# Routing a mixture-of-experts layer from un-normalised activations, with a rewritten slot search, first gather and w_out order

## What is computed

```
h = layer_norm(ALPHA * x + m @ wo, g1, b1)                      # 1024 wide
g_prob = softmax(h @ w_group + b_group)                         # 4 groups, top 1
e_logits = (h @ w_router + b_router)[chosen group]              # 4 experts, top 2
wts = softmax(top 2 logits) * g_prob[chosen group]
y = sum over 16 experts of combine[:, e] * (silu(h @ w_gate[e]) * (h @ w_up[e])) @ w_down[e]
out = layer_norm(ALPHA * h + y, g2, b2)
```

## Time and profile before

| | us |
|---|---|
| median of 3 timed runs | 973.34 |
| timed runs | 973.19, 973.34, 979.06 |
| profiled execution, its own time | 978.55 |
| its span | 976.7 |
| TensorE busy | 857.7 (88%) |
| VectorE busy | 544.1 (56%) |
| ScalarE busy | 438.2 (45%) |
| GpSimd busy | 163.3 (17%) |
| mean granted TensorE clock | 0.935 of full |

### The profile page before, as it was taken

How to read it: one execution, slowest core, us unless ns; L and a number is a source line. 1 busy time by engine, 2 the same in 40 slices (tenths; PEclk the granted TensorE clock), 3 DMA queues, 4 the chain that set the end, 5 groups by cost and what they waited for, 6 DMA issues and landing times.

```text
span 976.7 us, 13661 instructions
## 1 busy us (share of the span) xinstructions
PE 857.7 (88%) x5313; PEld 758.9 (78%) x5313; DVE 544.1 (56%) x622; ACT 438.2 (45%) x551; POOL 163.3 (17%) x137
## 2 busy tenths in 40 slices
PE   4999897889798999999998998368999999999930
PEld 4999896667588999999996676357888888888820
DVE  4121347656652332333334332828999999999927
ACT  3222322654643332233314112136878778788722
POOL 0094024312210000000000332100211112111012
PEclk9999999999978999999999997569999999999975
DMA  7323114700101312221224235778999999999744
GB/s 293 118 87 102 69 53 143 253 0 1 44 8 52 139 60 102 102 94 62 99 86 138 80 139 209 296 284 314 384 379 403 393 388 404 384 398 404 218 83 136
DMA packets 35530, 180.76 MB, mean 185 GB/s; under 512 B 3575, under 2 KB 11399, under 8 KB 19134
## 3 DMA queue, kind: packets, MB, share of 16 engines
q1 hardware_dynamic: 30246, 161.38, 43.4%
q0 software_dynamic: 5248, 18.91, 7.5%
HBM read 166.77 MB, written 17.94 MB: 189 GB/s over the span
## 4 chain that ended last, share of the span: by engine, by line
PE 79%; DVE 8%; DMA 4%; ACT 4%; issue 3%; POOL 0%; SPq 0%; POOLq 0%; ACTq 0%; DVEq 0%
PE ps L1024 8%; PE ps L1025 8%; PE ps L1026 8%; PE ps L1287 6%; PE ps L1289 6%; PE ps L1288 6%; PE ps L863 4%; PE ps L864 4%; PE ps L865 4%; PE ps L1314 3%; PE ps L1316 3%; PE ps L1315 3%; PE ps L1190 3%; PE ps L1217 2%; PE ps L1216 2%
## 5 line engine op out<-in xcount | busy, mean ns | idle before, releaser
L1681 DVE TENSOR_TENSOR elo<-eraw,ehi 128x2048 fp32r<-128x2048 f32 x96 | 218.2, 2291 | 29.9 <-ACT ehi L742 28.1
L742 ACT ACTIVATE ehi<-eraw 128x2048 fp32r<-128x2048 f32 x96 | 183.0, 1916 | 28.3 <-PE ps L1289 16.1
L1372 DVE TENSOR_TENSOR wlo<-raw,whi 128x2432 fp32r<-128x2432 f32 (+1 forms) x25 | 63.4, 2535 | 154.8 <-ACT whi L504 154.8
L1024 PE MATMUL ps<-xhi,whi 128*128 128x260 f32 x384 | 110.5, 288 | 3.5 <-DVE wlo L1546 3.5
L1025 PE MATMUL ps<-xhi,wlo 128*128 128x260 f32 x384 | 110.2, 287 | 0.0
L1026 PE MATMUL ps<-xlo,whi 128*128 128x260 f32 x384 | 110.1, 287 | 0.0
L1287 PE MATMUL ps<-ehi,xethi 128*128 128x512 f32 x256 | 103.1, 403 | 5.0 <-issue 5.0
L1289 PE MATMUL ps<-elo,xethi 128*128 128x512 f32 x256 | 101.3, 396 | 0.0
L1288 PE MATMUL ps<-ehi,xetlo 128*128 128x512 f32 x256 | 101.2, 395 | 0.0
L504 ACT ACTIVATE whi<-raw 128x2432 fp32r<-128x2432 f32 (+1 forms) x25 | 52.4, 2094 | 91.0 <-PE ps L1026 91.0
L1024 PEld LDWEIGHTS ps<-xhi,whi 128*128 128x128 f32 x384 | 74.3, 194 | 3.7 <-DVE wlo L1546 3.7
(11 more groups left out here) (324 smaller groups left out, 1874.9 us busy)
## 6 DMA issues: line engine op xcount, KB each, us to landing
eraw<-w_gate_in SPq DMA_DIRECT2D x32, 1024.0 KB, 13.2
eraw<-w_up_in SPq DMA_DIRECT2D x32, 1024.0 KB, 14.8
eraw<-w_down_in SPq DMA_DIRECT2D x32, 1024.0 KB, 14.3
raw<-wm_in SPq DMA_DIRECT2D x16, 1216.0 KB, 5.2
raw<-wz_in SPq DMA_DIRECT2D x8, 1024.0 KB, 5.9
raw<-wo_in SPq DMA_DIRECT2D x4, 1024.0 KB, 4.9
h_dram<-hall POOLq DMA_DIRECT2D x5, 416.0 KB, 3.4
f_dram<-h_dram SPq DMA_DIRECT2D x1, 2080.0 KB, 9.7
```

The costliest lines, as they stand in the source:

```text
L742: ac.activation(ehi[s % 3][:, :], eraw[s][:, :], ACT.Copy).then_inc(ehi_ok, 1)
L1024: pe.matmul(out, cols(whi[s], q), mh, start=k == 0, stop=False)
L1681: ve.tensor_tensor(elo[s % 3][:, :], eraw[s][:, :], ehi[s % 3][:, :].bitcast(F32), ALU.subtract)\
```

## The change

- **Router.** `ln1_g` and `ln1_b` are loaded as 16 rows of 128, transposed once, and multiplied into the router weights: `wgb[:, 0] = g * w`, `wgb[:, 1] = b * w`. Their sums over the 1024 channels come from 8 products; `wrt` becomes `g*w - mean`, `brow` the bias row. Since the mean is taken out of the weights, the logits of the un-normalised `hall` need only a factor 1/sigma per token, which `logit(t)` applies. TensorE transposes tile t as soon as it is summed (`h_sum`) in place of finished.
- **Order on TensorE.** Tiles 0 and 1 go through w_out together, k-block by k-block (`first_two`); the last tile is made in two column halves, with logits and transposes of tiles 2 to 4 in between (`halves_of_last`).
- **w_out.** VectorE's split of its second piece stands one step after the first, ahead of the rest of the last merge step.
- **Slot lists.** A slot is the rank itself, in 16 lists; `rowhot` is made in two halves; everything on overflow is taken out: the count (`overflow_count`) stands behind expert 1 on VectorE, the lists (`overflow_lists`) behind the branch.
- **Gain and bias of tile 4**, the two VectorE steps `lng`, `lnb`, stand behind the choice of the experts; the splits of expert 0's first weights stand behind the slot search. A Sigmoid of one column on ScalarE makes the table load earlier.
- **Loads.** One down piece comes early; of the rest of the pieces and the copy to `f_dram`, none is issued before the first gather has landed. The second gather waits for the first.

```diff
-            sp.wait_ge(h_sum, TT)
+            sp.wait_ge(h_sum, TT + 1)
+            sp.dma_start(rcon[:, :], a["route_consts"]).then_inc(rc_in, 16)
             expert_piece(2, 2, wu[0, 0], True)
-            sp.dma_start(rcon[:, :], a["route_consts"]).then_inc(rc_in, 16)
             for n in range(2):
                 expert_piece(6 + n, 6 + n, wu[1, n], True)
+            expert_piece(8, 8, wd[0, 0], True)
             sp.wait_ge(h_done, TT - 1)
             sp.wait_ge(h_last, 2)
+            sp.wait_ge(h_sent, 16 * TT)
             expert_piece(3, 3, wu[0, 1], True)
-            sp.wait_ge(lg_ps, TT)
-            sp.wait_ge(h_sent, 16 * TT)
+            sp.wait_ge(xe_in[0], 16)
             for n in range(2):
                 expert_piece(4 + n, 4 + n, wg[1, n], True)
-            for n in range(2):
-                expert_piece(8 + n, 8 + n, wd[0, n], True)
+            expert_piece(9, 9, wd[0, 1], True)
             expert_piece(10, 10, wg[2, 0], True)
-            sp.wait_ge(slc_seen, 2)
+            expert_piece(11, 11, wg[2, 1], True)
             sp.dma_start(f_dram[0:T, :], h_dram).then_inc(f_init, 16)
...
+            ac.wait_ge(h_ps, TT + 1)
+            esplit(0, 0, 16, True)
+            esplit(1, 1, 16, True)
...
             ac.activation(m2[:, :], m2[:, :], ACT.Exp).then_inc(r_exp, 1)
+            ac.activation(eone[:, :], con[:, C_ONE:C_ONE + 1], ACT.Sigmoid)
+            esplit(2, 2, 16, True)
...
+            pe.transpose(ps[:, 7, 0:2 * KD], gb16[:, :], ident[0:2 * KD, 0:2 * KD]).then_inc(fold_ps, 1)
             with pe.Fori(1, KD) as i:
                 merge(i)
 
+            pe.wait_ge(fold_ok, 2)
+            for k in range(KD):
+                last = pe.matmul(ps[:, 7, 64:104].rearrange("p (u n) -> p u n", u=2), con[:, C_ONE:C_ONE + P],
+                                 wgb[:, :, k, :], start=k == 0, stop=k == KD - 1)
+            last.then_inc(fold_ps, 1)
...
+            def first_two():
+                pe.wait_ge(m_hi, KD - 1)
+                pe.wait_ge(m_lo, KD - 1)
+                for k in range(KD):
+                    if k % 2 == 0:
                         pe.wait_ge(lo_split, N_O + k // 2 + 1)
...
+                    if k == KD - 1:
+                        pe.wait_ge(m_hi, KD)
+                        pe.wait_ge(m_lo, KD)
+                    for t in range(2):
+                        if k == 0:
+                            pe.wait_ge(m_step, 4 * (KD - 1) + 1 + t)
+                        block(t, k)
...
+            def halves_of_last():
+                t = TT - 1
+                mt = slice(t * TR, t * TR + TR)
+                pe.wait_ge(h_sum, t - 1)
+                for h in range(2):
+                    out = ps[0:TR, 2 * (t % 2) + h, :]
+                    for k in range(KD):
+                        if h == 1 and k == KD - 3:
+                            logits(t - 1)
+                            turn(t, 0)
                         pe.matmul(out, mhi[:, k, mt], wohi[:, k, h * 512:h * 512 + 512], start=k == 0, stop=False)
...
+                    last.then_inc(h_ps, 1)
+                    if h == 0:
+                        logits(t - 2)
+                        turn(t - 1)
...
+            def turn(t, half=None):
+                if half is None:
+                    pe.wait_ge(h_sum, t + 1)
                 else:
-                    pe.wait_ge(h_last, 2)
+                    pe.wait_ge(h_sum, t + half + 1)
                 if t:
                     pe.wait_ge(ht_out, t)
-                for k in range(KD):
+                for k in range(KD) if half is None else range(4 * half, 4 * half + 4):
                     last = pe.transpose(ps[:, 4 + k // 4, (k % 4) * TR:(k % 4) * TR + TR],
                                         hall[:, t, k * P:k * P + P], ident[0:TR, 0:TR])
...
+            first_two()
+            turn(0)
+            project(2)
+            logits(0)
+            turn(1)
+            project(3)
+            logits(1)
+            turn(2)
+            halves_of_last()
+            turn(TT - 1, 1)
...
+                    wo_split(1)
                 ve.wait_ge(m_step, 4 * i + 2)
...
+            ve.wait_ge(fold_ps, 1)
+            for n in range(2):
+                ve.tensor_tensor(wgb[:, n, :, :], wrt[:, :, :],
+                                 ps[:, 7, KD * n:KD * n + KD].rearrange("p (k a) -> p k a", a=1).broadcast_to([P, KD, 20]),
+                                 ALU.mult).then_inc(fold_ok, 1)
             with ve.Fori(1, KD - 1) as i:
                 merge(i, True)
             merge(KD - 1, False)
-            for j in range(1, 4):
+            for j in range(2, 4):
                 wo_split(j)
+            ve.wait_ge(fold_ps, 2)
+            ve.scalar_tensor_tensor(wrt[:, :, :], ps[:, 7, 64:84].rearrange("p (a n) -> p a n", a=1).broadcast_to([P, KD, 20]),
...
+            t = TT - 1
+            x, ls = hall[:, t, :], l1stat[t][0:TR]
+            ve.wait_ge(xrow_in[t % 2], 16 * (t // 2 + 1) + 16)
+            for h in range(2):
+                ve.wait_ge(h_ps, t + h + 1)
+                summed(t, slice(512 * h, 512 * h + 512))
+                ve.wait_ge(h_sum, t + h + 1)
+                stats(x, ls, h)
+                if h == 0:
+                    for n in range(TT - 2):
+                        logit(n)
+            ve.wait_ge(h_stat, 4 * t + 2)
+            ve.bn_aggr(ls[:, 12:14], ls[:, 0:12]).then_inc(h_stat, 1)
+            ve.wait_ge(h_stat, 4 * t + 3)
+            ve.tensor_scalar(ls[:, 14:15], ls[:, 13:14], EPS, None, ALU.add).then_inc(h_stat, 1)
+            logit(TT - 2)
+            ve.wait_ge(h_root, t + 1)
+            for n in range(4):
+                factor(n, ls, h_fac, 5 * t)
+            factor(4, ls, h_fac, 5 * t)
+            logit(TT - 1)
+            ve.wait_ge(rd, count[0])
...
+            ve.wait_ge(ln_in, 32)
+            ve.wait_ge(h_nrm, TT)
+            ve.tensor_tensor(x, x, lng[0:TR, :], ALU.mult).then_inc(h_last, 1)
+            ve.wait_ge(h_last, 1)
+            ve.tensor_tensor(x, x, lnb[0:TR, :], ALU.add).then_inc(h_last, 1)
...
+                                  rank.rearrange("p (a t) n -> p a t n", a=1).broadcast_to([TR, 2, TT, NE]), ALU.mult))
+            link(ve.tensor_reduce(slotf[:, :, :], picked[:, :, :, :], AX.X, ALU.add))
+            ve.tensor_tensor(chunkr[:, :, :, :], picks[:, :, :, :], wider(tokm[:, :, :], NE), ALU.mult)
+            ve.wait_ge(rc_in, 16)
+            row = rcon[0:TR, G_ROW:G_ROW + CAP]
+            for c in range(2):
+                ve.tensor_tensor(rowhot[:, c:c + 1, :, :], along(row, CAP, 1), wider(slotf[:, c:c + 1, :], CAP),
+                                 ALU.is_equal).then_inc(list_ok, 1)
...
+            link(ve.tensor_copy(rankc[:, :, :], rank))
+            link(ve.tensor_copy(tots[:, :], total))
+            ve.tensor_tensor(chunkw[:, :, :, :], picks[:, :, :, :], wider(w12[:, :, :], NE), ALU.mult).then_inc(list_ok, 1)
+            esplit(0, 0, True)
+            ve.wait_ge(slot_ps, 2)
+            ve.tensor_copy(wslot[:, 0:NE], ps[:, 7, P:P + NE]).then_inc(wslot_ok, 1)
+            link(ve.tensor_copy(ltri[:, :, :], rcon[0:TR, G_LT:G_LT + NE * NE].rearrange("p (a e) -> p a e", a=NE)))
             esplit(1, 1, True)
...
+            def overflow_count():
+                link(ve.tensor_scalar(oc[:, :], tots[:, :], float(CAP), None, ALU.is_gt))
+                for m in range(2, TT):
+                    link(ve.scalar_tensor_tensor(oc[:, :], tots[:, :], float(CAP * m), oc[:, :], ALU.is_gt, ALU.add))
+                link(ve.tensor_tensor(ocl[:, :, :], oc[:, :].rearrange("p (a e) -> p a e", a=1).broadcast_to([TR, NE, NE]),
...
             expert(0, 1)
+            overflow_count()
             with ve.Fori(1, NE // 2 - 1) as i:
...
+                if c == 1:
+                    gp.wait_ge(xe_in[0], 16)
                 gp.indirect_dma_start(out=xe[q][:, :], out_offset=None, in_=h_dram,
```

300 lines of the change are left out of this document (172 added, 128 removed).

## The result

The changed kernel takes **950.46 us** (median of four runs, 947.77 to 953.48) beside 973.27 for the kernel before (973.02 to 979.06): a ratio of 0.9746 over the runs, 95% interval 0.9712 to 0.978 (the two medians alone give 0.9766). The forecast was 952.5, with 944 to 961. The profiled executions took 978.55 and 953.48 us, 25.1 apart (spans 976.7 and 951.6, mean granted clock 0.935 and 0.950).

What follows compares the result with a forecast made beforehand. TensorE is the chain for 79% of the span, so edits pay only where it waits or runs at 1.2 GHz. Gains of 24.3 less 1.5 and 2 make 20.8 us, from 973.34 to 952.5, range 944 to 961.

Steps and rivals of the forecast that it cites:

- the second term: Last tile's sum to logits: 15.1 us before, 3.8 after, 11.3 us gained; the choice of experts keeps its 4.7 us.
- 1. w_out: Start and end of w_out: last tile's sum at 592.8 against 595.59, 3 us earlier (0 to 4.5).
- one spell at 1.2 GHz, as there is one before: In w_out, small products thin out the array's work; the low clock costs eight matmuls by 0.2, 1.6 us.
- no gap: Tiles 0 and 1 in w_out: pieces are split by the time their k-blocks are wanted; end at 547.7.
- 3. Choice to first expert: End of `both` to first expert matmul: 30.3 us before, 20.3 after, gather landing in 6; 10.0 us gained.
- rival (c): The first gather is not faster: 12.9 us stays, 4.1 less gained, time 956.6 us; chance 0.08.
- 4. The loop: Expert loop: the overflow count loses 1.5 us (0 to 2.8), supply of weight pieces 2 us (0 to 10).
- (a): Tighter fit: no 1.2 GHz spell in w_out, weight products at full clock, count and supply hidden; 945 us; chance 0.18.
- (b): Supply becomes the bound of the late experts: 8 to 10 us come back, time 959.5 us; chance 0.17.
- (d): Slower: all 26 us of transfer come back in the loop and the count costs 2.8; 978 us; chance 0.03.
- landmark signs: Among them: last sum near 593, logits 3.8 later, gather landing in 6, TensorE gap of 1 to 3 in expert 2.
- the signs that it would be wrong: TensorE waiting for `elo` over many experts, `h_dram` store or gather above 10 us, long 1.2 GHz in w_out.

Runs made afterwards that it cites:

- the control: The changed kernel run once more, unaltered: 950.31 us, ratio 0.9766 to the kernel before.

## Why the prediction was right, and where it was not

**It was right in total** (952.5 forecast, 950.46 measured): 20.8 us were forecast, the medians are 22.8 apart, and the changed part of the two profiles gained some 22.5. Part of the agreement is luck. w_out gave 2.15 us more than forecast and the search 1.65 less, and in the loop two misses of about the same size cancel. Only the second term held both in size and in mechanism.

**1. w_out: 3 us forecast, 5.15 measured; a size.** Counted from the merge step, the first matmul starts 5.76 us behind it; the forecast had 525.6 - 519.69 = 5.9. Tiles 0 and 1 then take 22.45 us (522.84 to 545.29, where the first transposes start) for 22.1. The difference is in the last part. The forecast put one spell at 1.2 GHz there, 1.6 us, and four tiles' logits at 1.64; the clock stayed at 1.00, and the logits took 1.40, 4 x 0.24 = 1.0 less. Together 2.6, of which some lost tenths take 0.4 back. The step that failed is "one spell at 1.2 GHz, as there is one before". The trace of before has in fact two spells of about eight matmuls in w_out: one from 539.2 to 542.6, behind the waits of 2.97 us and, for the last piece, 2.77; and one from 583.6 to 587, behind a tile's transposes, a wait for their copy and its logits (TensorE's timeline of before; the matmuls of the second row and its neighbours are 0.43 us apart):

```profile
581.10 1.64 PE L1234 MATMUL ps<-wrt,ht 128*104 128x20 f32 x16 [0.95 <-ACT ht L721]
...
584.40 0.63 PE L1215 MATMUL ps<-wohi,mhi 128*104 128x512 f32 x1
```

The changed kernel, with twice as many tiles' small products in w_out, has neither spell. It makes a tile's logits after the next tile's products, so that TensorE has no wait between transposes and logits; its start has no wait either, and the experiment that only starts late has a spell of thirteen matmuls. So the waits are what it lacks, and the small products it has. That a wait of 0.95 us was the cause of the second spell was not tried, and the same wait at 566.6 had no spell behind it. The step "no gap" held, but its reason was only half of it: the early landing of the last piece, on which the forecast rested it, costs nothing when undone alone, since the pairing of the tiles covers the same wait. Only with both undone do 6.0 us come back.

**2. Sum to logits: 11.3 forecast, 11.7 measured.** The logits are there 3.4 us behind the sum (forecast 3.8), and the choice takes the same 4.7. The experiments split the 11.7, if their parts can be added: 5.1 come from transposing what is not yet normalised; gain and bias, no longer ahead of the logits, are 2.5 (two steps of 1.23); 0.9 comes from putting tile 3's logits and half of tile 4's transposes among w_out's last products, which costs w_out 1.8; and what is left, 11.7 - 5.1 - 2.5 - 0.9 = 3.2, goes to the order in which tiles 2 to 4 are transposed and to the last sum by halves. That last part was not tried by itself.

**3. Choice to first expert: 10.0 forecast, 8.35 measured.** This is the step that failed in kind. "With the queue nearly empty ... landing 3.4 to 4 later ... It just misses being the limit": it took 8.24, and was the limit. SyncE issued `rcon` and four pieces, 4 MB, from 588.55 to 591.8, and these keep the DMA engines at over 320 GB/s from 592.4 to 602.6; the forecast counted the piece that was moved away, and not the four that stayed. Issued at 598.67, the store landed 10.9 us behind `both`, where the forecast has 6.2 to 6.8, and GpSimd issued the gather at 11.75 in place of 7.1. All else in the term held: slots 6.8 behind `both` forecast, 6.6 measured to their start; the gather 6 forecast, 5.80; landing to first matmul 4.4 in both. The sum with the real store is 11.75 + 5.80 + 4.4 = 22.0. With the pieces out of the store's way the forecast's own path appears, 19.75 for 20.3. The row of before that the forecast set aside, 7.41 us for this same store, was of the same kind: it landed at 611.55, 0.03 us behind a piece issued 0.2 us ahead of it.

The Trainium skill (DMA: Bandwidth & Descriptors, "Queues, rings and completion order") has the DMA engines take turns between queue rows, and rival (c) drew from it that the hold buys little. The trace agrees with the turns. The clearest row is of the kernel before: its gather went out at 628.40, when the last piece had been in since 626.44, and still took 12.91 us, beside a copy issued at 628.75 and pieces issued behind that, so it was slowed by transfers that were issued later. From 630 to 636 SyncE's queue moved 2.10 MB there in 63 packets, some 33 KB each, and the gather's 0.26 MB in another 63; without the hold the changed kernel issues the copy 2.6 us behind the gather and behind five pieces, and the gather takes 9.1. That the large packets of the copy made the difference fits turns by packet, but was not tried. What the trace does not bear out is the conclusion, that holding back buys little: it bought 3.3 us of gather. How far the same hold would have brought the 12.91 us down was not tried, since the old kernel was not run with a hold.

**4. The loop: 3.5 lost forecast, 3.1 measured, by another sum.** The count cost 1.5, as forecast. Supply cost nothing in place of 2. The forecast let the start of the loop take up 8 us of transfer; by the windows the changed kernel moved 22 us at 384 and 35 at 406 GB/s, 22.7 MB, between 618 and 675, where the kernel before moved 20 at 262 and 35 at 339, 17.1 MB, in 55 us. Allowing for the two us more, that is some 5 MB or 12.5 us taken up, not 8, and so nothing was left over. The landing times of the pieces went about as forecast, near 18 early in the loop (670 to 700) and near 28 at 820 to 850, and the limit is where it was suspected, but between 1 and 3 MB further on. The other 1.6 us is a last down product of 8.71 us in place of 7.12, at a granted clock of 0.81 behind TensorE's wait of 1.89 us. It is not the change's: the same product takes 7.1 in the control and four other variants and 8.7 in the rest, with the same wait of 1.89 or 1.90 us ahead of it (with 3 MB held, 9.4 behind a wait of 2.85); before it, too, had that wait and took 7.12.

**The rivals.** (a), tighter, holds for the clock in w_out and for supply, not for the weight products (4.45 us as before) and the count. (b) and (d), supply: not seen in the changed kernel, seen in small when 3 MB more were held. (c): the gather was faster. The landmark signs given in the forecast came out (logits 3.8 and 3.4, gather 6 and 5.8, gap in expert 2 of 1 to 3 and 1.28), but for "behind `xetlo` with VectorE busy ahead of it" and the time at which the gather leaves. Of the signs that it would be wrong none came: the store took 8.24 us and the gather 5.80, under the 10 named.

The Trainium skill's 425 GB/s for long streams (same page, "Measured") was set against 397 in the trace. Both are right, for different stretches. What the DMA engines moved from 760 to 790 in the changed kernel, in 40 slices of 0.75 us (DMA view):

```profile
GB/s 415 426 426 426 431 426 432 426 426 426 426 426 448 404 421 300 295 317 300 322 317 393 426 426 437 404 453 382 442 410 442 437 415 448 415 426 437 404 366 300
```

The trace agrees with the page's figure where pieces run alone or beside a gather. From 771 to 776, while an expert's accumulating store to `f_dram` moves, it is 295 to 322, and this pulls the mean of a whole round down to 392 at a share of 1.02. The forecast was right to plan with the mean of the mix. That supply cost nothing comes from the start of the loop, not from a faster stream.
